# Order of states, inputs and lag copies in the state space group loop, and where its power vectors lie

## The chip, the cores and the metric

The kernel runs on one core of one Trainium2 chip. Five engines run programs of their own and meet only at semaphores: TensorE (PE, with its weight loads shown as PEld), VectorE (DVE), ScalarE (ACT), GpSimd (POOL) and SyncE (SP). The metric is the device time of one execution in microseconds. The kernel before took 3051.56 us, the median of three runs that lay between 3043.96 and 3056.59 us.

## The reference

Two networks follow each other on 256 tokens of width 1024. The first has two layers (an mLSTM or RG-LRU mixer with cross-attention, and a feed-forward block that gathers expert rows). The second has two layers of feed-forward, mixer, feed-forward. The change lies in the mixer of the second network's first layer, a diagonal complex state space model with 64 groups of 16 channels and 64 states. Cut to what matters:

```
u = (h @ w_in).reshape(bsz, seq, 64, 16)
abar = exp(dt * a)                                  # complex, one per state
bu   = einsum('blgh,gph->blgp', u, f * b)           # inputs
st   = scan(abar, bu)                               # states over the sequence
y    = Re(einsum('blgp,ghp->blgh', st, c)) + d_skip * u
z    = gelu(y) * sigmoid(gelu(y) @ w_glu + b_glu)
out  = z @ w_out
```

## The kernel before, in words

The sequence of 256 tokens is cut into 64 steps of 4 tokens. What passes inside a step of four goes through "lag" matrices, what passes from step to step goes through a scan of 64 columns. The 4096 states lie as 128 partitions x 32 columns, and the loop handles 4 of the 32 columns at a time: 8 groups, `for g in range(S5_G + 1)`, with the end of group g - 1 in round g. A complex state turns by an angle at each step. The kernel turns inputs back by the angle, scans with the real magnitude alone, and turns the result forward again.

Ahead of the loop stands a front part. `dve_s5_params` works out vectors of 128x32: f (V_FR, V_FI) and the powers 1 to 4 of abar (V_AR, V_AI), most of them in the SBUF buffer skT. `dve_times` multiplies the b tables by f and by three powers on DVE (four calls of four instructions), `c_power` the c tables by powers 1 and 2 on DVE and by 3 and 4 on POOL. ACT meanwhile copies the columns of u into place (`u4_rows`, L1484). It then waits for the b tables, builds the first matrices (`act_s5_bbz`, L1508) and copies the third part of u. PE's first round opens with 48 small matmuls that are there only to keep it active (6 in later rounds).

In round g each engine runs its program in the order in which it is written:
- PE: `drive(g)` (6 matmuls to keep active, then 16 that give the inputs s.v g), `rows_b(g+1)` (L1406), `lags(g)` (the tile s.k g; it needs the c matrices that POOL copied), `outputs(g-1)` (into acc; it needs state g-1 from POOL and the lag copies of g-1 from DVE).
- DVE: t1, t2 of group g (L1777, L1778, the inputs turned back), q1, q2 of group g-1 (L1784, L1785, the scan turned forward), four lag copies of group g (L1499), eight scans of group g (L1791).
- POOL: the inputs of group g (L1642, L1644), the states of group g-1 (L1649, L1650), the c matrices for group g+1 (`pool_s5_cp`, L1604, which waits until outputs(g-1) has read the buffer), the angle of group g+2 (L1611), and, after ACT has rounded it (L1521, L1523), the turn (L1616).
- ACT: the weights of drive(g+1) (L1515), matrices of group g+2 (L1508), rounding, and the sines of group g+2 (L1531 to L1537), which wait for q2 of group g.

PSUM has eight banks. `ps` has four, which all tiles take in turn, so each tile of a round waits until the tile four earlier has been read: s.k g+1 waits for the lag copies of group g. `acc` has the other four. In the front part nothing uses them; in the loop outputs(g) fills half of bank g // 2.

The buffers and constants that the change names: `area(...)` is a piece of the SBUF buffer arena, `s5v(k)` is vector k of the state vectors, S5_J is 32.

Of the kernel before, what the change touches and what calls it, by code (L numbers as in the profile page):

```python
# [14 lines left out]
ALU = mybir.AluOpType  # L15
# [141 lines left out]
def build(nc, A, out, known):  # L157
# [6 lines left out]
    with ctx:  # L164
# [1453 lines left out]
        def pool_s5():  # L1618

            pool.wait_ge(dve_steps, count_of("x mid01"))  # L1620
            pool_s5_loads()
            pool.wait_ge(dve_steps, count_of("angle4"))
            pool_s5_ang(0)
            pool_s5_turn(0)
            pool.wait_ge(act_steps, count_of("cpu 0"))
            pool.wait_ge(dve_steps, count_of("s5 powers"))
            c_power(pool, PO, 3, p_tmp1, p_tmp2)
            pool_s5_ang(1)
            pool_s5_turn(1)
            c_power(pool, PO, 4, p_tmp1, p_tmp2)  # L1630
            pool.memset(cp, 0.0).then_inc(pool_steps, PO.step())
            pool.wait_ge(pool_steps, PO.n)
            pool.wait_ge(dve_steps, count_of("c powers"))
            pool_s5_cp(0)
            pool_s5_cp(1)
            for g in range(S5_G + 1):
                b = g % 2
                if g < S5_G:
                    if g >= 2:
                        pool.wait_ge(dve_steps, count_of(f"scan {g - 2}"))  # L1640
                    pool.wait_ge(dve_steps, count_of(f"t1 {g}"))
                    pool.tensor_tensor(w_in[:, b, 0, :, :], w_t1[:, b, 0, :, :], w_t1[:, b, 1, :, :], ALU.add).then_inc(pool_steps, PO.step(f"in re {g}"))  # L1642
                    pool.wait_ge(dve_steps, count_of(f"read s.v{g}"))
                    pool.tensor_tensor(w_in[:, b, 1, :, :], w_t2[:, b, 1, :, :], w_t2[:, b, 0, :, :], ALU.subtract).then_inc(pool_steps, PO.step(f"in im {g}"))  # L1644
                if g:
                    if g >= 3:
                        pool.wait_ge(pe_steps, count_of(f"s.y {g - 3}"))
                    pool.wait_ge(dve_steps, count_of(f"s.q {g - 1}"))
                    pool.tensor_tensor(w_st[:, 1 - b, 0, :, :], w_q1[:, 1 - b, 0, :, :], w_q1[:, 1 - b, 1, :, :], ALU.subtract).then_inc(pool_steps, PO.step())  # L1649
                    pool.tensor_tensor(w_st[:, 1 - b, 1, :, :], w_q2[:, 1 - b, 0, :, :], w_q2[:, 1 - b, 1, :, :], ALU.add).then_inc(pool_steps, PO.step(f"state {g - 1}"))  # L1650
                if g and g + 1 < S5_G:
                    pool_s5_cp(g + 1)
                if g + 2 < S5_G:
                    pool_s5_ang(g + 2)
                    pool_s5_turn(g + 2)

        def of_states(k):

            return s5v(k).unsqueeze(1).unsqueeze(3).to_broadcast([P, 2, S5_J, 16])

        def c_power(eng, E, k, t1, t2):

            eng.tensor_tensor(t1, cpu[:, 0, :, :, :], of_states(V_AR[k]), ALU.mult).then_inc(sems[E.who], E.step())
            eng.tensor_tensor(t2, cpu[:, 0, :, :, :], of_states(V_AI[k]), ALU.mult).then_inc(sems[E.who], E.step())
            eng.wait_ge(sems[E.who], E.n)
            eng.tensor_tensor(cpu[:, k, 0, :, :], t1[:, 0, :, :], t2[:, 1, :, :], ALU.add).then_inc(sems[E.who], E.step())
            eng.tensor_tensor(cpu[:, k, 1, :, :], t1[:, 1, :, :], t2[:, 0, :, :], ALU.subtract).then_inc(sems[E.who], E.step())
            eng.wait_ge(sems[E.who], E.n)

        def dve_times(re_out, im_out, src, ar, ai):  # L1670

            dve.tensor_tensor(d_tmp1, src, of_states(ar), ALU.mult).then_inc(dve_steps, VE.step())
            dve.tensor_tensor(d_tmp2, src, of_states(ai), ALU.mult).then_inc(dve_steps, VE.step())
            dve.wait_ge(dve_steps, VE.n)
            dve.tensor_tensor(re_out, d_tmp1[:, 0, :, :], d_tmp2[:, 1, :, :], ALU.subtract).then_inc(dve_steps, VE.step())
            dve.tensor_tensor(im_out, d_tmp1[:, 1, :, :], d_tmp2[:, 0, :, :], ALU.add).then_inc(dve_steps, VE.step())
            dve.wait_ge(dve_steps, VE.n)

        def dve_s5_params():
# [64 lines left out]
            for k, (i, j) in ((2, (1, 1)), (3, (2, 1)), (4, (2, 2))):  # L1744
# [6 lines left out]
                two(V_AI[k], V(V_AI[k]), V(V_TMP2), ALU.add)  # L1751
                done()
            found["s5 powers"] = (VE.who, VE.n)

        def dve_s5():
            n = "mid01"
            dve_pre(n)
            dve_s5_params()
            dve.wait_ge(s5_b, count_of("s5 b loaded"))
            dve_times(bbk[:, 3, 0, :, :], bbk[:, 3, 1, :, :], b_raw, V_FR, V_FI)  # L1760
            for k in range(1, S5_L):
                dve_times(bbk[:, 3 - k, 0, :, :], bbk[:, 3 - k, 1, :, :], bbk[:, 3, :, :, :], V_AR[k], V_AI[k])
                found["b powers"] = (VE.who, VE.n)
            dve.wait_ge(act_steps, count_of("cpu 0"))
            for k in (1, 2):
                c_power(dve, VE, k, d_tmp1, d_tmp2)
            found["c powers"] = (VE.who, VE.n)
            u4_rows(VE, 3)
            for g in range(S5_G + 1):
                b = g % 2  # L1770
                if g < S5_G:
                    dve.wait_ge(act_steps, count_of(f"cs {g}"))
                    v = cs[:, b, :, :, :]
                    o = tile_of(VE, f"s.v{g}").rearrange("p (a q c) -> p a q c", a=2, q=4)
                    if g >= 2:
                        dve.wait_ge(pool_steps, count_of(f"in im {g - 2}"))
                    dve.tensor_tensor(w_t1[:, b, :, :, :], o, v, ALU.mult).then_inc(dve_steps, VE.step(f"t1 {g}"))  # L1777
                    dve.tensor_tensor(w_t2[:, b, :, :, :], o, swapped(v), ALU.mult).then_inc(dve_steps, VE.step(f"read s.v{g}"))  # L1778
                if g:
                    v = cs[:, 1 - b, :, :, :]  # L1780
                    dve.wait_ge(dve_steps, count_of(f"scan {g - 1}"))
                    if g >= 3:
                        dve.wait_ge(pool_steps, count_of(f"state {g - 3}"))
                    dve.tensor_tensor(w_q1[:, 1 - b, :, :, :], w_sc[:, 1 - b, :, :, :], v, ALU.mult).then_inc(dve_steps, VE.step())  # L1784
                    dve.tensor_tensor(w_q2[:, 1 - b, :, :, :], w_sc[:, 1 - b, :, :, :], swapped(v), ALU.mult).then_inc(dve_steps, VE.step(f"s.q {g - 1}"))  # L1785
                if g < S5_G:
                    dve_s5_lags(g)
                    for part in range(2):
                        dve.wait_ge(pool_steps, count_of(f"in {('re', 'im')[part]} {g}"))
                        for q in range(4):  # L1790
                            dve.tensor_tensor_scan(w_sc[:, b, part, q, :], s5v(V_MAG4)[:, 4 * g + q:4 * g + q + 1].to_broadcast([P, S5_C]),  # L1791
                                                   w_in[:, b, part, q, :], 0.0, ALU.mult, ALU.add).then_inc(dve_steps, VE.step(f"scan {g}"))
            dve.wait_ge(act_steps, count_of("y gelu 1"))
            for q in range(3):
                for l in range(S5_L):
                    dst, src = y_rows(l, q, 0)
                    dve.tensor_copy(dst, src).then_inc(dve_steps, VE.step("y dve 0"))
# [12 lines left out]
            dve_post(n, acc_rows, 1.0, tmp_s5, "ffn02")  # L1810
# [277 lines left out]
```

## Time and profile before

| | |
|---|---|
| median of 3 runs | 3051.56 us (3043.96 to 3056.59) |
| profiled execution, its own time | 3055.92 us |
| span of the profile | 3054.2 us |
| PE busy | 2530.4 us, 83% |
| DVE busy | 1679.8 us, 55% |
| POOL busy | 1062.8 us, 35% |
| ACT busy | 799.8 us, 26% |
| mean granted TensorE clock | 0.908 |

The profile is one execution. Busy time counts instructions of an engine; its idle time before an instruction is put down to what released it last. The granted clock is the share of TensorE's full 2.4 GHz: 1.00 in a stretch is 2.4 GHz, 0.50 is 1.2 GHz, and values between are stretches that hold some of both. The state space mixer takes the span from about 2034 to 2264 us: its front part up to 2095, the loop to 2203, then the gate and output products.

### The profile page before, as it was taken

The page shows a single profiled execution, that of the slowest core. Times are in us where ns is not written, and L with a number is a line of the kernel's source. Part 1 is how long each engine was busy: PE and PEld are TensorE (multiplying, and loading weights), DVE is VectorE, ACT ScalarE, POOL GpSimd, SP SyncE. Part 2 cuts the span into 40 slices and gives each one's busy share as a digit, 9 for nine tenths or more (in the row PEclk, how much of TensorE's full clock was granted, in tenths as well). Part 3 has the DMA queues.
Part 4 walks back from the last instruction along what each step waited for, and adds up shares of the span by engine and source line. Part 5 has one row for each costly group of instructions (what it writes and reads, how often), then busy time and mean ns, then how long its engine had stood idle before and what let it go on. Part 6 is the DMA issues. An engine that isn't in the chain of part 4 may idle for free.

```text
span 3054.2 us, 29765 instructions
## 1 busy us (share of the span) xinstructions
PE 2530.4 (83%) x10910; PEld 1737.0 (57%) x10910; DVE 1679.8 (55%) x3410; ACT 799.8 (26%) x1499; POOL 1062.8 (35%) x1155
## 2 busy tenths in 40 slices
PE   8978777778778986877777778988889989997898
PEld 7847322223324664332222338976759979875797
DVE  0135666676753337766667635647525545464454
ACT  1111221212211412222121124334324343324332
POOL 0002777777772016777777740015300000000000
PEclk9979888998899998888888988998799989998899
DMA  6415999999995349999999973551036545521353
GB/s 226 152 62 204 404 409 409 407 405 403 409 404 195 115 154 399 409 407 408 400 409 403 409 301 124 200 162 53 16 116 193 193 135 190 202 88 42 125 188 116
DMA packets 322209, 766.87 MB, mean 251 GB/s; under 512 B 22064, under 2 KB 172496, under 8 KB 322064
## 3 DMA queue, kind: packets, MB, share of 16 engines
q0 software_dynamic: 150208, 546.77, 45.5%
q1 hardware_dynamic: 170576, 217.69, 21.9%
q8 instruction: 88, 1.44, 0.2%
q10 hardware_dynamic: 1280, 0.50, 0.1%
q14 instruction: 57, 0.47, 0.0%
HBM read 763.83 MB, written 1.05 MB: 250 GB/s over the span
## 4 chain that ended last, share of the span: by engine, by line
PE 53%; DVE 15%; DMA 14%; POOL 10%; issue 6%; ACT 2%; ACTq 0%; DVEq 0%; POOLq 0%
PE ps L267 29%; PE acc L267 23%; DMA arena<-in_peer_u,arena 13%; POOL arena L1029 9%; DVE arena L994 2%; DMA arena<-in_peer_v,arena 1%; DVE arena L925 1%; DVE arena L931 1%; DVE arena L927 1%; DVE arena L929 1%; DVE arena L923 1%; PE ps L325 1%; DVE arena L957 1%; DVE arena L961 0%; DVE arena L963 0%
## 5 line engine op out<-in xcount | busy, mean ns | idle before, releaser
L267 PE MATMUL acc<-arena 128*128 128x512 f32 (+2 forms) x2362 | 1044.9, 598 | 331.6 <-ACT arena L918 278.9
L267 PEld LDWEIGHTS acc<-arena 128*128 128x128 f32 x2362 | 464.1, 206 | 908.4 <-issue 579.7
L1029 POOL DMA_INDIRECT arena<-in_peer_u,arena x512 | 487.2, 952 | 420.2 <-DVE arena L967 242.1
L1029 POOL DMA_INDIRECT arena<-in_peer_v,arena x512 | 482.0, 941 | 207.1 <-issue 126.6
L299 DVE TENSOR_TENSOR lo_ring<-ring,hi_ring 128x2048 fp32r<-128x2048 f32 x132 | 302.0, 2289 | 329.7 <-ACT hi_ring L291 329.4
L994 DVE CUSTOM_DVE_ANT_0 arena<-arena,ps 128x1024 f32<-128x1024 f32 x256 | 306.7, 1219 | 214.3 <-DMA arena<-in_peer_u,arena 213.7
L994 DVE CUSTOM_DVE_ANT_0 arena<-arena,acc 128x1024 f32<-128x1024 f32 x256 | 305.6, 1219 | 191.6 <-DMA arena<-in_peer_u,arena 190.7
L267 PE MATMUL ps<-x_hi,hi_ring 128*128 128x256 f32 x1408 | 401.5, 285 | 11.1 <-DVE x_lo L1210 11.1
L267 PE MATMUL ps<-x_hi,lo_ring 128*128 128x256 f32 x1408 | 400.2, 284 | 0.0
L267 PE MATMUL ps<-x_lo,hi_ring 128*128 128x256 f32 x1408 | 398.0, 283 | 0.0
L291 ACT CAST hi_ring<-ring 128x2048 fp32r<-128x2048 f32 x132 | 250.6, 1900 | 435.8 <-PE ps L267 333.7
L267 PE MATMUL ps<-x_fm,ring 128*128 128x256 f32 (+2 forms) x1568 | 350.3, 385 | 6.7 <-ACT acc L981 2.2
L267 PEld LDWEIGHTS ps<-x_fm,ring 128*128 128x128 f32 (+2 forms) x1568 | 291.4, 187 | 60.9 <-issue 3.7
L267 PEld LDWEIGHTS ps<-x_hi,hi_ring 128*128 128x128 f32 x1408 | 270.1, 192 | 12.6 <-DVE x_lo L1210 12.6
L267 PEld LDWEIGHTS ps<-x_lo,hi_ring 128*128 128x128 f32 x1408 | 269.5, 191 | 0.0
L267 PEld LDWEIGHTS ps<-x_hi,lo_ring 128*128 128x128 f32 x1408 | 268.9, 191 | 0.0
L918 ACT ACTIVATE arena<-ident,arena 128x128 f32<-128x128 f32 x512 | 153.0, 387 | 311.0 <-DVE arena L1006 311.0
L267 PE MATMUL acc<-hi_ring,a_hi 128*128 128x512 f32 x352 | 138.5, 393 | 0.0
L267 PE MATMUL acc<-hi_ring,a_lo 128*128 128x512 f32 x352 | 138.0, 392 | 0.0
L267 PE MATMUL acc<-lo_ring,a_hi 128*128 128x512 f32 x352 | 138.0, 392 | 0.0
L912 ACT ACTIVATE arena<-arena 128x16 f32<-128x16 f32 x32 | 6.9, 216 | 392.4 <-DVE arena L994 392.4
L1967 POOL DMA_DIRECT2D rowb<-in_norm_post x6 | 3.4, 565 | 289.9 <-DVE stat L1249 270.4
(341 smaller groups left out, 2249.1 us busy)
## 6 DMA issues: line engine op xcount, KB each, us to landing
ring<-in_ffn_w SPq DMA_DIRECT2D x132, 1024.0 KB, 5.4
ring<-in_peer_w_q SPq DMA_DIRECT2D x16, 1024.0 KB, 5.4
ring<-in_mlstm_w_in SPq DMA_DIRECT2D x12, 1024.0 KB, 5.2
arena<-in_peer_u,arena POOLq DMA_INDIRECT x512, 8.9
arena<-in_peer_v,arena POOLq DMA_INDIRECT x512, 8.6
ring<-in_cv_w_in SPq DMA_DIRECT2D x8, 1024.0 KB, 5.5
ring<-in_rglru_w_in SPq DMA_DIRECT2D x8, 768.0 KB, 4.8
ring<-in_w_out SPq DMA_DIRECT2D x5, 1024.0 KB, 4.9
```

The costliest lines, as they stand in the source:

```text
L267: return pe.matmul(o, l, r, start=first, stop=last)
L291: act.copy(parts(name)[0], flat(name, ring, i % RING)).then_inc(act_steps, AC.step("hi " + name))
L299: dve.tensor_tensor(lo, flat(name, ring, i % RING), hi.bitcast(F32), ALU.subtract).then_inc(dve_steps, VE.step("lo " + name))
L325: i = pe.transpose(o[:, 256 * k + 128 * t:256 * k + 128 * t + 128], src(t, 2 * c + k), ident[:, :])
L918: act.activation(diag[:, k, :], ident[:, :], ACT.Copy, scale=coef[b][:, k:k + 1]).then_inc(act_steps, AC.step(f"diag {i}.{j - 1}.{k}"))
L923: dve.max(out_v[:, a], s).then_inc(dve_steps, VE.step())
L925: dve.max_index(out_i[:, a], out_v[:, a], s).then_inc(dve_steps, VE.step())
L927: dve.match_replace(s, out_v[:, a], s, NEG).then_inc(dve_steps, VE.step())
L929: dve.max(out_v[:, b], s).then_inc(dve_steps, VE.step())
L931: dve.max_index(out_i[:, b], out_v[:, b], s).then_inc(dve_steps, VE.step())
L994: dve.tensor_tensor_reduce(r, r, x_row(t), 1.0, 0.0, ALU.mult, ALU.add, dots[b][:, k:k + 1]).then_inc(dve_steps, VE.step(f"u used {g}"))
L1029: pool.indirect_dma_start(ring_[:, g % slots, :], None, table, bass.IndirectOffsetOnAxis(ix[j % 4][:, k:k + 1].bitcast(U32), 0), element_o ...
```

## The change

Three things change, all in the state space mixer. In the diff the increments of the engines' own semaphores, which end most lines, are cut off.

1. In each round DVE does q1, q2 of group g-1 first, then t1, t2 of group g, then the scans of group g, and the lag copies of group g last. In each round POOL does the two state instructions of group g-1 ahead of the two input instructions of group g.
2. `dve_times`, and `c_power` where DVE runs it, read their coefficient vectors from acc bank 3 in PSUM (`near_states`). One new DVE copy of 128x288 brings the nine vectors there from skT. POOL still reads them in SBUF.
3. The first temporary of these DVE functions, d_tmp1, lies in acc banks 1 and 2, not in arena.

```
-        d_tmp1, d_tmp2 = area(0, 2, S5_J, 16), area(1024, 2, S5_J, 16)
+        d_tmp1 = acc[:, 1:3, :].rearrange("p a (j h) -> p a j h", h=16)
+        d_tmp2 = area(1024, 2, S5_J, 16)
...
             for g in range(S5_G + 1):
                 b = g % 2
+                if g:
+                    if g >= 3:
+                        pool.wait_ge(pe_steps, count_of(f"s.y {g - 3}"))
+                    pool.wait_ge(dve_steps, count_of(f"s.q {g - 1}"))
+                    pool.tensor_tensor(w_st[:, 1 - b, 0, :, :], w_q1[:, 1 - b, 0, :, :], w_q1[:, 1 - b, 1, :, :], ALU.subtract)
+                    pool.tensor_tensor(w_st[:, 1 - b, 1, :, :], w_q2[:, 1 - b, 0, :, :], w_q2[:, 1 - b, 1, :, :], ALU.add)
                 if g < S5_G:
...
-                if g:
-                    if g >= 3:
-                        pool.wait_ge(pe_steps, count_of(f"s.y {g - 3}"))
-                    pool.wait_ge(dve_steps, count_of(f"s.q {g - 1}"))
-                    pool.tensor_tensor(w_st[:, 1 - b, 0, :, :], w_q1[:, 1 - b, 0, :, :], w_q1[:, 1 - b, 1, :, :], ALU.subtract)
-                    pool.tensor_tensor(w_st[:, 1 - b, 1, :, :], w_q2[:, 1 - b, 0, :, :], w_q2[:, 1 - b, 1, :, :], ALU.add)
...
+        def near_states(k):
+
+            return acc[:, 3, S5_J * (k - 7):S5_J * (k - 7) + S5_J].unsqueeze(1).unsqueeze(3).to_broadcast([P, 2, S5_J, 16])
+
         def c_power(eng, E, k, t1, t2):
...
-            eng.tensor_tensor(t1, cpu[:, 0, :, :, :], of_states(V_AR[k]), ALU.mult)
-            eng.tensor_tensor(t2, cpu[:, 0, :, :, :], of_states(V_AI[k]), ALU.mult)
+            states = near_states if E is VE else of_states
+            eng.tensor_tensor(t1, cpu[:, 0, :, :, :], states(V_AR[k]), ALU.mult)
+            eng.tensor_tensor(t2, cpu[:, 0, :, :, :], states(V_AI[k]), ALU.mult)
...
-            dve.tensor_tensor(d_tmp1, src, of_states(ar), ALU.mult)
-            dve.tensor_tensor(d_tmp2, src, of_states(ai), ALU.mult)
+            dve.tensor_tensor(d_tmp1, src, near_states(ar), ALU.mult)
+            dve.tensor_tensor(d_tmp2, src, near_states(ai), ALU.mult)
...
             found["s5 powers"] = (VE.who, VE.n)
+            dve.wait_ge(dve_steps, count_of("acc ffn00 read"))
+            dve.tensor_copy(acc[:, 3, 0:288], skT[:, :, :].rearrange("p a b -> p (a b)")[:, 224:512])
+            dve.wait_ge(dve_steps, VE.n)
...
             for g in range(S5_G + 1):
                 b = g % 2
+                if g:
+                    v = cs[:, 1 - b, :, :, :]
+                    dve.wait_ge(dve_steps, count_of(f"scan {g - 1}"))
+                    if g >= 3:
+                        dve.wait_ge(pool_steps, count_of(f"state {g - 3}"))
+                    dve.tensor_tensor(w_q1[:, 1 - b, :, :, :], w_sc[:, 1 - b, :, :, :], v, ALU.mult)
+                    dve.tensor_tensor(w_q2[:, 1 - b, :, :, :], w_sc[:, 1 - b, :, :, :], swapped(v), ALU.mult)
                 if g < S5_G:
...
-                if g:
-                    v = cs[:, 1 - b, :, :, :]
-                    dve.wait_ge(dve_steps, count_of(f"scan {g - 1}"))
-                    if g >= 3:
-                        dve.wait_ge(pool_steps, count_of(f"state {g - 3}"))
-                    dve.tensor_tensor(w_q1[:, 1 - b, :, :, :], w_sc[:, 1 - b, :, :, :], v, ALU.mult)
-                    dve.tensor_tensor(w_q2[:, 1 - b, :, :, :], w_sc[:, 1 - b, :, :, :], swapped(v), ALU.mult)
-                if g < S5_G:
-                    dve_s5_lags(g)
                     for part in range(2):
                         dve.wait_ge(pool_steps, count_of(f"in {('re', 'im')[part]} {g}"))
                         for q in range(4):
                             dve.tensor_tensor_scan(w_sc[:, b, part, q, :], s5v(V_MAG4)[:, 4 * g + q:4 * g + q + 1].to_broadcast([P, S5_C]),
                                                    w_in[:, b, part, q, :], 0.0, ALU.mult, ALU.add)
+                    dve_s5_lags(g)
```

A round of the loop on DVE, in the kernel before (ps is the tile read, arena the SBUF buffer; L1777 and L1778 are t1 and t2, L1784 and L1785 q1 and q2, L1499 the lag copies, L1791 the scans):

```order
L1777 TENSOR_TENSOR arena<-ps,arena 128x512 [waits pool_steps,pe_steps,act_steps]
L1778 TENSOR_TENSOR arena<-ps,arena 128x512
L1784 TENSOR_TENSOR arena<-arena 128x512 [waits pool_steps,dve_steps]
L1785 TENSOR_TENSOR arena<-arena 128x512
L1499 COPY arena<-ps 32x512 [waits pe_steps]
L1499 COPY arena<-ps 32x4x96
L1791 SCALAR_TENSOR_TENSOR arena<-mix_fm,arena 128x64 [waits pool_steps]
L1791 SCALAR_TENSOR_TENSOR arena<-mix_fm,arena 128x64 x3
```

The same round on DVE in the changed kernel (q1 and q2 are L1785 and L1786, t1 and t2 L1793 and L1794, the scans L1798, the lag copies L1500):

```order
L1785 TENSOR_TENSOR arena<-arena 128x512 [waits pool_steps,dve_steps]
L1786 TENSOR_TENSOR arena<-arena 128x512
L1793 TENSOR_TENSOR arena<-ps,arena 128x512 [waits pool_steps,pe_steps,act_steps]
L1794 TENSOR_TENSOR arena<-ps,arena 128x512
L1798 SCALAR_TENSOR_TENSOR arena<-mix_fm,arena 128x64 [waits pool_steps]
L1798 SCALAR_TENSOR_TENSOR arena<-mix_fm,arena 128x64 x3
L1500 COPY arena<-ps 32x512 [waits pe_steps]
L1500 COPY arena<-ps 32x4x96
```

The forward turn of the last group no longer stands behind the wait for PE's tile s.v g, and the lag copies no longer stand ahead of the scans.

On POOL, from the c matrices of one round to those of the next, before (L1604 the c matrices, L1611 the angle, L1616 the turn, L1642 and L1644 the inputs, L1649 and L1650 the states):

```order
L1604 COPY arena<-arena 64x20x16
L1611 TENSOR_TENSOR arena<-mix_fm,t_row 128x256 [waits act_steps,pool_steps]
L1616 TENSOR_TENSOR arena<-arena 128x256 [waits act_steps]
L1642 TENSOR_TENSOR arena<-arena 128x256 [waits dve_steps]
L1644 TENSOR_TENSOR arena<-arena 128x256 [waits dve_steps]
L1649 TENSOR_TENSOR arena<-arena 128x256 [waits dve_steps,pe_steps]
L1650 TENSOR_TENSOR arena<-arena 128x256
L1604 COPY arena<-arena 64x20x16 [waits pool_steps,pe_steps]
```

And in the changed kernel (L1605 the c matrices, L1612 the angle, L1617 the turn, L1643 and L1644 the states, L1649 and L1651 the inputs):

```order
L1605 COPY arena<-arena 64x20x16
L1612 TENSOR_TENSOR arena<-mix_fm,t_row 128x256 [waits act_steps,pool_steps]
L1617 TENSOR_TENSOR arena<-arena 128x256 [waits act_steps]
L1643 TENSOR_TENSOR arena<-arena 128x256 [waits dve_steps,pe_steps]
L1644 TENSOR_TENSOR arena<-arena 128x256
L1649 TENSOR_TENSOR arena<-arena 128x256 [waits dve_steps]
L1651 TENSOR_TENSOR arena<-arena 128x256 [waits dve_steps]
L1605 COPY arena<-arena 64x20x16 [waits pool_steps,pe_steps]
```

The states, for which PE waits, now come two instructions earlier on POOL, and the inputs two later. PE's and ACT's programs keep their order.

On DVE in the front part, the first call of dve_times in the changed kernel, behind the last vectors:

```order
L1690 TENSOR_TENSOR mix_fm<-mix_fm,skT 128x32
L1761 COPY acc<-skT 128x288 [waits dve_steps]
L1678 TENSOR_TENSOR acc<-arena,acc 128x1024 [waits s5_b,dve_steps]
L1679 TENSOR_TENSOR arena<-arena,acc 128x1024
L1681 TENSOR_TENSOR arena<-acc,arena 128x512 [waits dve_steps]
L1682 TENSOR_TENSOR arena<-acc,arena 128x512
```

Before, L1672 and L1673 stood for the two products and L1675 and L1676 for the sum and difference, with arena and skT in the place of each acc, and without the copy.

## Rows read from the trace of the kernel before

**Rows 1.** Windows: busy us of each engine (x), granted clock, DMA share, GB/s.
```profile
2034.00:2095.00 61.00, 38.97 (x178) 33.66 (x178) 54.43 (x95) 33.74 (x98) 33.24 (x22) 0.79 0.40 112
2095.00:2203.00 108.00, 99.00 (x655) 85.97 (x654) 65.03 (x157) 38.75 (x88) 49.03 (x78) 0.77 0.03 11
```

**Rows 2.** The same view, three shorter stretches of the loop.
```profile
2102.00:2112.20 10.20, 10.20 (x88) 7.83 (x86) 7.40 (x18) 3.52 (x8) 4.22 (x6) 1.00 0.00 0
...
2114.80:2127.50 12.70, 12.70 (x60) 11.59 (x60) 4.18 (x13) 3.48 (x9) 4.55 (x8) 0.50 0.01 2
2127.50:2139.10 11.60, 11.32 (x98) 9.28 (x96) 8.09 (x18) 5.10 (x13) 6.78 (x11) 1.00 0.01 1
```

**Rows 3.** Timeline of PE: start, us, line, names, xcount, idle before and releaser.
```profile
2114.76 0.66 PE L267 MATMUL acc<-mix_fm,arena 128*128 128x64 f32 x2 [2.55 <-DVE arena L1499]
...
2119.91 1.49 PE L267 MATMUL ps<-ident 128*128 128x256 bf16 x6
...
2130.02 0.41 PE L267 MATMUL acc<-mix_fm,arena 128*128 128x64 f32 x2 [0.24 <-POOL arena L1650]
...
2132.72 0.82 PE L267 MATMUL ps<-ident 128*128 128x256 bf16 x6
...
2136.08 0.62 PE L267 MATMUL ps<-arena 128*32 128x128 f32 x4
...
2140.97 0.58 PE L267 MATMUL acc<-mix_fm,arena 128*128 128x64 f32 x2 [1.91 <-POOL arena L1650]
...
2183.96 0.82 PE L267 MATMUL ps<-ident 128*128 128x256 bf16 x6
...
2201.63 3.73 PE L267 MATMUL ps<-x_fm,ring 128*128 128x256 f32 x8
```

**Rows 4.** Timeline of POOL in the round that ends with the 1.91 us wait.
```profile
2132.95 1.85 POOL L1604 COPY arena<-arena 64x320 f32<-64x320 f32 x4 [3.08 <-PE acc L267]
2134.88 0.61 POOL L1611 TENSOR_TENSOR arena<-mix_fm,t_row 128x256 f32<-128x256 f32 x1
2136.47 0.72 POOL L1616 TENSOR_TENSOR arena<-arena 128x256 f32<-128x256 f32 x1 [0.98 <-ACT arena L1523]
2137.16 1.17 POOL L1642 TENSOR_TENSOR arena<-arena 128x256 f32<-128x256 f32 x1
...
2139.42 0.72 POOL L1649 TENSOR_TENSOR arena<-arena 128x256 f32<-128x256 f32 x1
```

**Rows 5.** Timeline of DVE in the same round.
```profile
2135.36 0.69 DVE L1777 TENSOR_TENSOR arena<-ps,arena 128x512 f32<-128x512 f32 x1 [1.73 <-issue]
...
2137.67 1.21 DVE L1785 TENSOR_TENSOR arena<-arena 128x512 f32<-128x512 f32 x1
2139.10 2.02 DVE L1499 COPY arena<-ps 32x512 f32<-32x512 f32 x4 [0.22 <-PE ps L267]
2141.15 1.56 DVE L1791 TENSOR_TENSOR_SCAN arena<-mix_fm,arena 128x64 f32<-128x64 f32 x8
```

**Rows 6.** Groups by line, DVE, 2060 to 2095: busy us, mean ns, idle before.
```profile
L1673 DVE TENSOR_TENSOR arena<-arena,skT 128x1024 f32<-128x1024 f32 x4 | 8.1, 2020 | 0.0
...
L1663 DVE TENSOR_TENSOR arena<-arena,skT 128x1024 f32<-128x1024 f32 x2 | 2.4, 1224 | 0.1
...
L1666 DVE TENSOR_TENSOR arena<-arena 128x512 f32<-128x512 f32 x2 | 1.4, 692 | 0.1
```

**Rows 7.** Timelines of DVE, ACT and PE in the front part.
```profile
2034.55 2.36 DVE L1245 TENSOR_TENSOR arena<-acc,rowb 128x1024 f32<-128x1024 f32 x2 [17.96 <-PE acc L267]
...
2060.61 1.22 DVE L1672 TENSOR_TENSOR arena<-arena,skT 128x1024 f32<-128x1024 f32 x1
...
2074.92 8.97 ACT L1484 COPY mix_fm<-ps 32x128 f32<-32x128 f32 x32
2087.09 1.68 ACT L1508 COPY arena<-arena 64x256 f32<-64x256 f32 x4 [3.20 <-DVE arena L1676]
...
2093.41 6.98 PE L267 MATMUL ps<-ident 128*128 128x256 bf16 x48 [2.62 <-ACT mix_fm L1484]
```

More of the change, by code:

```diff
@@ L1637, in pool_s5 @@
                 b = g % 2
+                if g:
+                    if g >= 3:
+                        pool.wait_ge(pe_steps, count_of(f"s.y {g - 3}"))
+                    pool.wait_ge(dve_steps, count_of(f"s.q {g - 1}"))
+                    pool.tensor_tensor(w_st[:, 1 - b, 0, :, :], w_q1[:, 1 - b, 0, :, :], w_q1[:, 1 - b, 1, :, :], ALU.subtract).then_inc(pool_steps, PO.step())
+                    pool.tensor_tensor(w_st[:, 1 - b, 1, :, :], w_q2[:, 1 - b, 0, :, :], w_q2[:, 1 - b, 1, :, :], ALU.add).then_inc(pool_steps, PO.step(f"state {g - 1}"))
                 if g < S5_G:
@@ L1644, in pool_s5 @@
                     pool.tensor_tensor(w_in[:, b, 1, :, :], w_t2[:, b, 1, :, :], w_t2[:, b, 0, :, :], ALU.subtract).then_inc(pool_steps, PO.step(f"in im {g}"))
-                if g:
-                    if g >= 3:
-                        pool.wait_ge(pe_steps, count_of(f"s.y {g - 3}"))
-                    pool.wait_ge(dve_steps, count_of(f"s.q {g - 1}"))
-                    pool.tensor_tensor(w_st[:, 1 - b, 0, :, :], w_q1[:, 1 - b, 0, :, :], w_q1[:, 1 - b, 1, :, :], ALU.subtract).then_inc(pool_steps, PO.step())
-                    pool.tensor_tensor(w_st[:, 1 - b, 1, :, :], w_q2[:, 1 - b, 0, :, :], w_q2[:, 1 - b, 1, :, :], ALU.add).then_inc(pool_steps, PO.step(f"state {g - 1}"))
                 if g and g + 1 < S5_G:
@@ L1659, in of_states @@
             return s5v(k).unsqueeze(1).unsqueeze(3).to_broadcast([P, 2, S5_J, 16])
+        def near_states(k):
+            return acc[:, 3, S5_J * (k - 7):S5_J * (k - 7) + S5_J].unsqueeze(1).unsqueeze(3).to_broadcast([P, 2, S5_J, 16])
         def c_power(eng, E, k, t1, t2):
-            eng.tensor_tensor(t1, cpu[:, 0, :, :, :], of_states(V_AR[k]), ALU.mult).then_inc(sems[E.who], E.step())
-            eng.tensor_tensor(t2, cpu[:, 0, :, :, :], of_states(V_AI[k]), ALU.mult).then_inc(sems[E.who], E.step())
+            states = near_states if E is VE else of_states
+            eng.tensor_tensor(t1, cpu[:, 0, :, :, :], states(V_AR[k]), ALU.mult).then_inc(sems[E.who], E.step())
+            eng.tensor_tensor(t2, cpu[:, 0, :, :, :], states(V_AI[k]), ALU.mult).then_inc(sems[E.who], E.step())
             eng.wait_ge(sems[E.who], E.n)
@@ L1670, in dve_times @@
         def dve_times(re_out, im_out, src, ar, ai):
-            dve.tensor_tensor(d_tmp1, src, of_states(ar), ALU.mult).then_inc(dve_steps, VE.step())
-            dve.tensor_tensor(d_tmp2, src, of_states(ai), ALU.mult).then_inc(dve_steps, VE.step())
+            dve.tensor_tensor(d_tmp1, src, near_states(ar), ALU.mult).then_inc(dve_steps, VE.step())
+            dve.tensor_tensor(d_tmp2, src, near_states(ai), ALU.mult).then_inc(dve_steps, VE.step())
             dve.wait_ge(dve_steps, VE.n)
@@ L1753, in dve_s5_params @@
             found["s5 powers"] = (VE.who, VE.n)
+            dve.wait_ge(dve_steps, count_of("acc ffn00 read"))
+            dve.tensor_copy(acc[:, 3, 0:288], skT[:, :, :].rearrange("p a b -> p (a b)")[:, 224:512]).then_inc(dve_steps, VE.step())
+            dve.wait_ge(dve_steps, VE.n)
         def dve_s5():
@@ L1770, in dve_s5 @@
                 b = g % 2
+                if g:
[3 more added lines that the diff above has]
+                        dve.wait_ge(pool_steps, count_of(f"state {g - 3}"))
+                    dve.tensor_tensor(w_q1[:, 1 - b, :, :, :], w_sc[:, 1 - b, :, :, :], v, ALU.mult).then_inc(dve_steps, VE.step())
+                    dve.tensor_tensor(w_q2[:, 1 - b, :, :, :], w_sc[:, 1 - b, :, :, :], swapped(v), ALU.mult).then_inc(dve_steps, VE.step(f"s.q {g - 1}"))
                 if g < S5_G:
@@ L1778, in dve_s5 @@
                     dve.tensor_tensor(w_t2[:, b, :, :, :], o, swapped(v), ALU.mult).then_inc(dve_steps, VE.step(f"read s.v{g}"))
-                if g:
-                    v = cs[:, 1 - b, :, :, :]
-                    dve.wait_ge(dve_steps, count_of(f"scan {g - 1}"))
-                    if g >= 3:
-                        dve.wait_ge(pool_steps, count_of(f"state {g - 3}"))
-                    dve.tensor_tensor(w_q1[:, 1 - b, :, :, :], w_sc[:, 1 - b, :, :, :], v, ALU.mult).then_inc(dve_steps, VE.step())
-                    dve.tensor_tensor(w_q2[:, 1 - b, :, :, :], w_sc[:, 1 - b, :, :, :], swapped(v), ALU.mult).then_inc(dve_steps, VE.step(f"s.q {g - 1}"))
-                if g < S5_G:
-                    dve_s5_lags(g)
                     for part in range(2):
```

## The prediction

> **What bounds the kernel now.** I read the windows of the mixer first, to see what its stages are worth, then the timelines of PE, POOL and DVE side by side over two rounds, then the front part. The mixer's front part takes 61 us and its loop 108 of the span's 3054.2, and in neither is DMA a limit: its share in the loop is 0.03 [rows 1]. What stands behind the loop follows PE's own end of it, so a microsecond saved here should reach the end.
>
> In the loop PE looks nearly always busy (99.0 of 108 us), but the granted clock is 0.77 [rows 1]. The shorter windows show why: 10.2 us without a gap at clock 1.00, then a gap of 2.55 us, then 12.7 us at 0.50 (1.2 GHz), then 11.6 at 1.00 again [rows 2, 3]. Another gap, of 1.91 us, ends that fast stretch [rows 3], and the pattern stands three times more, with gaps of about 2 us. No stretch at the full clock in the loop ended without one; the first lasted about 15 us from its rise at 2097. So a gap costs twice: itself, and the slow stretch behind it.
>
> A round at the full clock needs from PE 3.36 us up to the lags (2132.72 to 2136.08), 2.98 us for them (to 2139.06: the next start less its wait of 1.91) and 2.70 us for the outputs (2130.02 to 2132.72): 9.04 us. Five rounds took 2183.96 - 2119.91 = 64.05 us, 12.81 each [rows 3].
>
> What makes the gap is POOL. It starts the c matrices 0.23 us into the round and ends them at 2.1; then come the angle, ACT's rounding and the turn, until 4.44; then the two inputs, 2.26 us (1.17 for what takes 0.72 alone), and the two states, after which PE goes on at 8.25 (2140.97), 1.91 late [rows 4, 3]. Beside the inputs DVE runs q1 and q2 at about 1.2 us each, where t1, of their size, takes 0.69 [rows 5].
>
> **The loop, part by part.** No instruction is added in a round and PE's and ACT's order stays. I count from the start of a round at the full clock.
>
> POOL's states move ahead of the inputs: 4.44 + 1.55 (2139.42 to 2140.97, states and PE's reaction) = 5.99, and PE wants them at 6.34. The gap goes, with 0.35 us to spare, if q2 is done by 4.44. The inputs, now behind, run from about 5.9 to 7.8 (1.9 us, between 1.44 and 2.26); of the eight scans (1.56 us) half are left then, until 8.6; the lag copies, 2.02 us, have their tile since 6.34 and end at 10.6; q1 and q2, 1.3 to 2.4 us, at 11.9 to 13.0, that is 2.9 to 4.0 in the next round [rows 3 to 5]. That is 0.4 to 1.5 before 4.44. What is queued behind q1 and q2 on DVE are t1, t2, and for them wait POOL's inputs: they end at 5.4 at the latest, and POOL is free at 5.9. PE's lags of the next group need the bank that the lag copies free at 10.6 - 9.04 = 1.6 and the c matrices at 2.1, both ahead of 3.36. ACT's sines wait for q2 and the turn; the turn is last, as before.
>
> So a round becomes 9.04 us by this; I take 9.3, because 0.35 us are eaten by one collision of POOL with DVE. First outputs: the lags of group 1 end at 2112.20, now the outputs follow at once and take 2.70 instead of the slow 5.15, so that the round ends at 2114.9, not 2119.91: 5.0 us. Five rounds: 5 x (12.81 - 9.3) = 17.5 us. The tail, from 2183.96 to 2201.63, is 17.67 us now [rows 3]. In the new order PE is done with outputs 6 after 2.4 + 2.98 + 2.7 = 8.1, but the last state comes after q2 of group 6 (3.5), two states (4.9), inputs (6.7), scans (7.6), copies (9.6), q1 and q2 (10.9), states: 12.4. The gap is over 4 us and the last outputs run slowly, 5.15: 17.5. The tail gives nothing. That gap's slow stretch may reach 2 us into the gate product, which now begins sooner behind it: minus 1 us. Loop: 5.0 + 17.5 - 1 = 21.5 us.
>
> **The front part.** The 24 DVE instructions of the power tables run from 2060.61 [rows 7]. The first ones collide with POOL's c powers: a 128x1024 product takes 2.02 us in the mean, and 1.22 where POOL does nothing, a 128x512 one 0.69 [rows 6]. The Trainium skill, page "SBUF — State Buffer", section "Who interferes with whom", has DVE's second SBUF input go through a read port that GpSimd shares, by an exclusive lock, and an instruction with one SBUF input contend with nobody; L1777, with one input in PSUM, keeps 0.69. In the new form each of the 24 has one SBUF input. A call of dve_times should take 2 x 1.22 + 2 x 0.69 = 3.8 us; four calls, 15.3, from 2061.1 to 2076.4, where before ACT got them at 2087.09.
>
> What is late next is ACT. Its columns of u run from 2074.92 to 2083.89, and start after POOL's turn of group 1. POOL loses its collisions too (an angle takes 0.61 alone [rows 4]); I estimate 2.1 us from that. ACT then ends at 2081.8, builds its matrices at once instead of waiting 3.20 us, and PE's 48 small matmuls start 5.3 us earlier than 2093.41 [rows 7]. DVE's c powers end at 2084 and its 16 copies of u near 2089, before the 2095 at which PE asks for them.
>
> No row shows DVE writing PSUM, nor reading it with one word repeated. The nearest row is L1245, 128x1024 from acc, two in 2.36 us [rows 7], so I take 1.22. The other end is the 2.02 of the collided form, for which a call takes 5.4 us and DVE's copies end near 2099: PE gets its inputs 4 us later than planned, and the front gives 1 us. Nothing bounds it below the uncollided form, since that is one pass over the same elements. The new copy of 128x288 lies between 0.4 and 0.7 us by the 0.69 of a 128x512 one; it is hidden, as DVE has 5 us to spare ahead of ACT.
>
> Sum: 21.5 + 5.3 = 26.8, say 27 us. The profiled execution took 3055.92 us, so it would take 3028.9. It lies 4.4 above the median of the runs; against 3051.56 this gives 3024.8, and I say 3025.
>
> **Rivals.** *The clock falls without a gap.* The Trainium skill, page "TensorE: Matmul & The Clock Gate", section "A second HAM failure mode: psum-queue depth-cycling", tells of a kernel whose clock went up and down because PE idled briefly between groups while it cycled through PSUM banks, as this loop does with its four. In this trace the window 2102 to 2112.2 speaks against it (the same small matmuls, clock 1.00, no gap), and that the outputs were not among them speaks for it. Then only the gaps go: 2.55 and four of about 1.7, 9 us, and with the front's 5.3 the time is 3051.6 - 14 = 3037.
>
> *The wait only moves.* POOL's and DVE's instructions with two SBUF inputs are 1.3 (q) + 1.6 (scans) + 1.85 + 0.61 + 0.72 + 1.45 + 1.44 = 9.0 us of a 9.04 us round. If each collides, the states come 0.7 to 1 us late each round and the clock keeps falling. By the lock that the skill's SBUF page describes this is what would happen if all of them took it; rows 4 and 5 show it for q against inputs, while POOL's copies took 1.85 us beside scans. Then the loop gives about 6 us, the front 5: 3041.
>
> *The front gives nothing*, PSUM forms being slow: 21.5 alone, 3030.
>
> *Slower.* The lag copies now stand behind the scans, which stand behind POOL's inputs, and PE's next lags need their bank. If the copies end more than 1.8 us later than I reckon, a gap opens ahead of the lags in every round. With a gap in each there is no fast stretch; a round at 1.2 GHz takes 1.85 x 9.04 = 16.7 us, against 12.81, and six rounds add 23 us, less 5 from the front: 3070. Against it speak the 1.8 us, and that a slow PE makes room for DVE.
>
> **Chances.** The forecast 0.60 (3020 to 3031), clock falls without a gap 0.17, the wait moves 0.08, no gain in front 0.10, slower 0.05. About 0.5%, 15 us, is what a measurement of this kernel can tell from no change. The forecast and the front's rival are faster than 3036.3, as is a third of the first rival: 0.76. The rest of the first two is within 0.5%: 0.19. Slower 0.05. The range that leaves out 2 in 10 reaches from 3016, where all of 32 us comes and the run is a quick one, to 3041.
>
> **What would show it.** In the changed profile PE's waits for POOL's states should be under 0.3 us in rounds 1 to 5 and the granted clock of the loop's first 70 us 1.00; a new gap of 4 us before the last outputs; L1678 and L1679 near 1.22 us, L1681 and L1682 near 0.69; ACT without a wait for the b tables. I am wrong if the clock falls in the middle of the loop behind no gap, if PE waits for the lag copies, or if L1678 takes 2 us.

## The result, and the profile after

The changed kernel took 3020.72 us, the median of four runs (3016.55 to 3022.94), against 3053.37 for four runs of the kernel before: ratio 0.9894, 95% interval 0.9879 to 0.9909, 32.6 us less. The forecast was 3025, 27 us less. Its profiled execution took 3019.64 us with a span of 3017.9, 36.3 less than before.

Where these 36.3 us went can be read from four marks in both timelines: the mixer's start (the first product of the post-norm ahead of it, L1245), PE's 48 small matmuls, the gate product, and the next L1245.

| us | before | after | less by | forecast |
|---|---|---|---|---|
| ahead of the mixer | 2034.55 | 2031.66 | 2.9 | 0 |
| front part, to the 48 matmuls | 58.86 | 52.15 | 6.7 | 5.3 |
| loop, to the gate product | 108.22 | 84.45 | 23.8 | 22.5 |
| gate and output products | 61.71 | 61.73 | 0.0 | -1 |
| behind the mixer | | | 2.9 | 0 |

The mixer gives 30.5 us of the 36.3. The stages around it hold the same instructions, and differ by 2.9 us on either side. No run ties these 5.8 us to the change, and the prediction did not count them.

PE's timeline after answers to [rows 3] (start, us, names, xcount, idle before and releaser):

```profile
2083.81 7.01 PE L267 MATMUL ps<-ident 128*128 128x256 bf16 x48 [3.50 <-ACT mix_fm L1485]
...
2096.27 0.83 PE L267 MATMUL ps<-ident 128*128 128x256 bf16 x6
...
2105.28 0.82 PE L267 MATMUL ps<-ident 128*128 128x256 bf16 x6
...
2111.94 0.41 PE L267 MATMUL acc<-mix_fm,arena 128*128 128x64 f32 x2 [0.32 <-POOL arena L1644]
...
2114.64 0.82 PE L267 MATMUL ps<-ident 128*128 128x256 bf16 x6
...
2150.64 0.82 PE L267 MATMUL ps<-ident 128*128 128x256 bf16 x6
...
2163.12 0.66 PE L267 MATMUL acc<-mix_fm,arena 128*128 128x64 f32 x2 [4.20 <-POOL arena L1644]
...
2168.26 3.73 PE L267 MATMUL ps<-x_fm,ring 128*128 128x256 f32 x8
```

One wait of 0.32 us is left in the middle; the five rounds from 2105.28 take 45.36 us, 9.07 each, where they took 64.05. The tail from 2150.64 takes 17.62 us, as before (17.67), with the forecast gap ahead of the last outputs. PE's gaps in the loop add up to 8.9 us before and to 4.5 after, so only 4.4 of the 23.8 us are idle time that went; the other 19.4 came from the clock. The windows view (busy us of PE, PEld, DVE, ACT, POOL, then granted clock, DMA share, GB/s) shows the clock:

```profile
2090.66:2153.00 62.34, 62.02 (x540) 53.73 (x538) 46.92 (x111) 34.77 (x81) 38.36 (x62) 1.00 0.01 1
...
2163.10:2174.00 10.90, 8.88 (x32) 7.63 (x32) 8.34 (x22) 4.45 (x6) 0.97 (x2) 0.57 0.26 98
2174.15:2200.40 26.25, 26.17 (x120) 22.72 (x120) 2.08 (x3) 2.56 (x7) 0.00 (x0) 1.00 0.36 120
```

The full clock, 2.4 GHz, now lasts 62 us in one piece, where [rows 2] had it change every 10 to 15 us. In the loop it falls only at the 4.20 us of the tail, and is back when the gate product goes on.

In the front part the groups by line on DVE (busy us, mean ns, idle before) answer to [rows 6]:

```profile
L1678 DVE TENSOR_TENSOR acc<-arena,acc 128x1024 f32<-128x1024 f32 x4 | 4.9, 1229 | 0.1
L1679 DVE TENSOR_TENSOR arena<-arena,acc 128x1024 f32<-128x1024 f32 x4 | 4.9, 1213 | 0.0
...
L1681 DVE TENSOR_TENSOR arena<-acc,arena 128x512 f32<-128x512 f32 x4 | 2.8, 692 | 0.1
...
L1761 DVE COPY acc<-skT 128x288 f32<-128x288 f32 x1 | 0.5, 461 | 0.0
```

POOL's timeline there; the same two instructions took 2.90 and 1.59 us before, beside DVE's instructions with two SBUF inputs:

```profile
2057.84 1.93 POOL L1669 TENSOR_TENSOR arena<-arena,skT 128x1024 f32<-128x1024 f32 x1 [4.69 <-DVE mix_fm L1690]
...
2061.74 1.27 POOL L1672 TENSOR_TENSOR arena<-arena 128x512 f32<-128x512 f32 x1
```

And ACT's, which answers to [rows 7]:

```profile
2068.46 8.99 ACT L1485 COPY mix_fm<-ps 32x128 f32<-32x128 f32 x32
2077.48 1.69 ACT L1509 COPY arena<-arena 64x256 f32<-64x256 f32 x4
```

ACT builds its matrices without a wait (3.20 us before), and its columns of u start 36.80 us after the mixer's start, where they started at 40.37.

### The profile page after: what moved, and what is told of

The parts are those of the page before. It is cut to its first block, busy times and chain, and to the rows that moved or that the text cites. A ratio compares the mean times of both kernels' runs of the same rounds, so it can differ in the third digit from the quotient of the medians.

```text
span 3017.9 us, 29767 instructions
## 1 busy us (share of the span) xinstructions
PE 2506.1 (83%) x10910; PEld 1716.1 (57%) x10910; DVE 1668.3 (55%) x3411; ACT 799.7 (26%) x1499; POOL 1050.5 (35%) x1155
## 4 chain that ended last, share of the span: by engine, by line
PE 54%; DVE 14%; DMA 13%; POOL 11%; issue 6%; ACT 2%; ACTq 0%; DVEq 0%; POOLq 0%
PE ps L267 30%; PE acc L267 24%; DMA arena<-in_peer_u,arena 12%; POOL arena L1029 10%; DVE arena L994 3%; DVE arena L925 1%; DVE arena L931 1%; DVE arena L927 1%; DMA arena<-in_peer_v,arena 1%; DVE arena L929 1%; PE ps L325 1%; DVE arena L923 1%; DVE arena L957 1%; DVE arena L1245 0%; ACT mix_fm L1485 0%
## 5 line engine op out<-in xcount | busy, mean ns | idle before, releaser
L267 PEld LDWEIGHTS acc<-arena 128*128 128x128 f32 x2362 | 457.1, 202 | 907.2 <-issue 579.3
```

What stands on the lines that cost most here:

```text
L267: return pe.matmul(o, l, r, start=first, stop=last)
```

## The experiments

The theory: PE's gap was POOL's, POOL's delay came from its order and from collisions with DVE, and the slow clock behind each gap cost more than the gap. The rivals: the clock falls for another reason; one of the two orders would have done; the front part's gain hangs on something else than the second SBUF input. The runs were made on several chips, and on two of them the kernel before took 3194 and 3207 us. So the experiments are compared by the mixer's stages between the four marks, where the same instructions take the same time on each (the 120 matmuls of the gate product at the full clock: 26.17 us on each). Where no ratio is given, the numbers are those of a single execution.

**Front part alone.** The loops of `pool_s5` and `dve_s5` are those of before, all else is the changed kernel.

> Only the front part is changed (vectors and first temporary in PSUM), the loop keeps the old order. Theory (DVE and POOL wait for each other at the SBUF port, ACT was held by the b tables): the front part, from the post-norm's first product to PE's 48 small matmuls, falls from 58.9 us to about 52.2, the loop stays at 108 +- 2 with its four gaps and slow stretches; total 6 to 7 us less than before, ratio 0.998. Rival (the front gain would have been eaten by PE's clock or a later wait, and the loop alone made the difference): front near 58, total unchanged.

Measured: ratio 0.9978 (0.9962 to 0.9994), front part 52.07 us, loop 108.04. The four gaps of the kernel before are all there (2.55, 1.88, 1.89 and 2.14 us; 2.55, 1.91, 1.89 and 2.14 before), and one of 0.88 us behind them, where 0.19 stood. The theory holds. In the profiled execution the gate part took 64.8 us instead of 61.7: the clock came back only within the gate product, whose 120 matmuls took 29.1 us instead of 26.2.

**Loop alone.** The other half: power tables in SBUF as before, the new orders.

> Only the loop's orders on DVE and POOL are changed, the power tables stay in SBUF. Theory: front 58.9 us as before, loop from 108.2 to about 84.5 us with rounds of 9.0 to 9.4 us at clock 1.00; total 23 to 24 us less than before, ratio 0.992. Rival (the two parts need each other, since an earlier DVE gives the loop its lead): the loop stays above 90 us.

Measured: ratio 0.9907 (0.9886 to 0.9928), front 58.89, loop 84.72, gate part 61.73. The two parts need nothing of each other: 58.86 - 52.07 = 6.8 and 108.22 - 84.72 = 23.5 us add to 30.3, and the changed kernel has 30.5.

**One engine's order alone.** First `pool_s5` as changed with `dve_s5` as before, then the other way round; the power tables as before in both.

> Only POOL's order in the loop is changed (states ahead of inputs), DVE's is old. Theory: q1, q2 come after t1, t2 and end near 5.0 to 5.3 us into a fast round, so the states end near 6.7 and PE waits 0.3 to 0.6 us a round instead of 1.9 in every second; if a gap so small leaves the clock alone the loop takes about 88 us. Rival (both orders are needed to close the gap): gaps of 1 us and more remain, the clock keeps falling, loop 100 us or more.

> Only DVE's order in the loop is changed (q1, q2 first, lag copies last), POOL's is old. Theory: the inputs no longer collide with q1, q2 and take 1.45 instead of 2.26 us, so the states end near 7.4 us into a fast round and PE waits about 1.0 us; loop between 92 and 105 us, with slow stretches if 1 us is enough to bring the clock down. Rival (DVE's order is what counts): gap gone, loop near 85 us.

Measured: with POOL's order alone the loop took 104.9 us, with DVE's alone 103.8. The second lies in the range of its theory, the first does not. PE's timeline with POOL's order alone:

```profile
2273.24 0.82 PE L267 MATMUL ps<-ident 128*128 128x256 bf16 x6
...
2280.53 0.41 PE L267 MATMUL acc<-mix_fm,arena 128*128 128x64 f32 x2 [0.95 <-POOL arena L1643]
...
2283.23 0.82 PE L267 MATMUL ps<-ident 128*128 128x256 bf16 x6
...
2290.45 0.41 PE L267 MATMUL acc<-mix_fm,arena 128*128 128x64 f32 x2 [0.88 <-POOL arena L1643]
...
2294.38 1.49 PE L267 MATMUL ps<-ident 128*128 128x256 bf16 x6
```

I had expected 0.3 to 0.6 us there and a clock that holds. The gap was 0.95 us, since q1 stands behind t1 and t2 and met POOL's turn (DVE's L1784 took 1.15 us), and the clock fell behind the second gap: the small matmuls at 2294.38 take 1.49 us instead of 0.82. So the rival was right here (it had asked for 1 us and more): both orders are needed. With DVE's order alone the inputs shrink from 1.17 to 0.73 us, as the theory says, and PE still waits 1.28 us in the middle (L1650, the states, end at 2281.48 and PE goes on at 2281.63), which brings the clock down in every second round. A gap of 0.9 to 1.3 us in place of 1.9 gave 3.3 and 4.5 us of 23.5.

**The gap filled.** The kernel before, its order untouched:

```
                 if g:
+                    if g < S5_G:
+                        keep_active(acc[:, 3, 256:512], 16)
                     outputs(g - 1)
```

> The kernel before, with 16 more of the small bf16 matmuls between a round's lags and its outputs, in rounds 1 to 7; no order is changed and no wait is removed. Theory (the slow clock is caused by the gaps and is two thirds of the loop's loss): at the full clock the 16 take 1.75 us of a gap of 1.9 that is there anyway, the clock stays at 1.00 in the middle of the loop, rounds take about 11 us and the loop 95 to 98 us instead of 108, though PE does more work. Rival (what was lost is PE's waiting itself, or the small matmuls bring the clock down anyway): the clock still falls and the loop takes 108 us or more.

Measured: loop 102.17 us, between the two. The windows say why:

```profile
2264.00:2279.00 15.00, 14.96 (x82) 12.06 (x83) 5.78 (x15) 6.84 (x17) 6.30 (x10) 0.59 0.00 1
2283.50:2327.00 43.50, 43.50 (x379) 37.27 (x378) 27.63 (x64) 20.29 (x48) 26.68 (x40) 1.00 0.01 1
```

In the first round 16 matmuls were too few, a gap of 0.70 us stayed and a slow stretch followed. From then on no gap was left and the clock stayed at 1.00 for all of the middle. Four rounds there took 10.87 us each, though PE did 1.8 us more work in each than in a kernel whose rounds took 12.81. This shows the price most clearly: no engine's work for the states was touched, the gaps were only filled, and the 1.9 us a round come from the clock alone.

**One gap put in.** The changed kernel, round 4 of POOL alone:

```
                     pool.wait_ge(dve_steps, count_of(f"s.q {g - 1}"))
+                    if g == 4:
+                        for _ in range(3):
+                            pool.tensor_tensor(w_st[:, 1 - b, 0, :, :], w_q1[:, 1 - b, 0, :, :], w_q1[:, 1 - b, 1, :, :], ALU.subtract)
+                            pool.wait_ge(pool_steps, PO.n)
```

> The changed kernel, with POOL's first state instruction done three times over ahead of itself in round 4 alone, 0.7 us each. Theory: one gap of about 2.1 us ahead of outputs 3, a slow stretch of 10 to 14 us behind it, and a loop of 84.5 + 2.1 + 5 to 6.5 = 91.5 to 93 us. Rival (the clock falls for another reason): only the 2.1 us, 86.6.

```profile
2255.00:2290.00 35.00, 34.67 (x300) 29.46 (x300) 27.57 (x64) 18.05 (x44) 21.78 (x36) 1.00 0.00 1
...
2293.10:2305.00 11.90, 11.86 (x56) 11.22 (x57) 6.47 (x16) 3.11 (x9) 6.58 (x11) 0.50 0.01 1
2306.00:2325.00 19.00, 19.00 (x164) 16.11 (x164) 12.08 (x31) 10.76 (x21) 9.68 (x17) 1.00 0.00 1
```

Measured: a gap of 2.30 us, 12 us at 1.2 GHz behind it, loop 92.96 us. That is 8.5 us more than the changed kernel for 2.3 us of idle time: the gap makes the clock fall, and the slow stretch costs about 6 us (0.3 of the rest is a longer gap in the tail, 4.53 us).

**Lag copies ahead of the scans again**, q1 and q2 still first (`dve_s5_lags(g)` moved back above the scans).

> The changed kernel with one part of the order undone: DVE's lag copies again ahead of the scans. Theory (PE waits for POOL's chain of c matrices, angle, turn and states, and DVE has over 1 us to spare): the loop stays within 1.5 us of 84.5. Rival (the copies have to be last, since the scans would then end too late for q1, q2 and the states): PE waits 0.5 us or more in each round and the loop takes 90 us or more.

Measured: loop 87.25 us, outside both numbers. PE waits 0.34 us in each round and the rounds are 9.38 us. POOL's and DVE's timelines of one of these rounds:

```profile
2280.92 2.56 POOL L1605 COPY arena<-arena 64x320 f32<-64x320 f32 x4 [1.71 <-PE acc L267]
2283.55 0.61 POOL L1612 TENSOR_TENSOR arena<-mix_fm,t_row 128x256 f32<-128x256 f32 x1
```

```profile
2281.54 0.76 DVE L1785 TENSOR_TENSOR arena<-arena 128x512 f32<-128x512 f32 x1
2282.22 0.93 DVE L1786 TENSOR_TENSOR arena<-arena 128x512 f32<-128x512 f32 x1
```

The end of the scans, q1 and q2 now run beside POOL's c matrices, which take 2.56 us instead of 1.75. The angle takes 0.61 us instead of 0.93 to 1.00, and in sum the states come about 0.4 us later. DVE had not run out of time: q2 ends 2.5 us into this round, before the 3.6 of the changed kernel. So the copies' place is worth 2.8 us because it decides which of POOL's instructions q1 and q2 meet. It is no condition for the full clock, which even held behind a first gap of 0.82 us.

**Vectors in PSUM, first temporary in SBUF.**

```
-        d_tmp1 = acc[:, 1:3, :].rearrange("p a (j h) -> p a j h", h=16)
-        d_tmp2 = area(1024, 2, S5_J, 16)
+        d_tmp1, d_tmp2 = area(0, 2, S5_J, 16), area(1024, 2, S5_J, 16)
```

> The changed kernel with the coefficient vectors in PSUM but the first temporary back in SBUF. Theory (it is the second SBUF input that makes DVE and POOL wait for each other): the products keep 1.22 us, the sums and differences, now with two SBUF inputs, take 0.9 to 1.6 us instead of 0.69 while POOL works, and the front part takes 52.5 to 54.5 us. Rival (PSUM for the vectors is all that matters): front 52.1 and all four at their times of the changed kernel.

```profile
L1681 DVE TENSOR_TENSOR arena<-arena 128x512 f32<-128x512 f32 x4 | 5.4, 1351 | 0.0
L1677 DVE TENSOR_TENSOR arena<-arena,acc 128x1024 f32<-128x1024 f32 x4 | 4.9, 1220 | 0.1
...
L1680 DVE TENSOR_TENSOR arena<-arena 128x512 f32<-128x512 f32 x4 | 4.8, 1200 | 0.1
```

Measured: front part 53.03 us, inside the range. The two products, one input in PSUM, keep 1.22 us beside POOL's work; the sum and difference, both inputs in SBUF again, take 1.20 and 1.35 us in the mean, where they take 0.69 and 0.68 with one in PSUM. The theory holds, and the rule of the Trainium skill's page "SBUF — State Buffer" ("Who interferes with whom"), that two SBUF inputs on DVE contend with GpSimd and one does not, agrees with this trace; the temporary's place is worth 0.9 us of the 6.7.

**A better version.** Two places stood out: PE spends 7 us on the 48 matmuls after it has been idle, since their bank comes free late, and the tail's 4.20 us gap.

```
-                keep_active(o, 48 if g == 0 else 6)
+                keep_active(o, 6)
...
-            rows_b(0)
             pe.wait_ge(dve_steps, count_of("acc ffn00 read"))
+            keep_active(acc[:, 0, :], 18)
+            rows_b(0)
+            keep_active(acc[:, 0, :], 46)
...
+                    if g == S5_G:
+                        keep_active(acc[:, 3, 256:512], 22)
                     outputs(g - 1)
```

In the tail version DVE also does, in round 7 alone, q1 and q2 of group 7 ahead of its lag copies.

> The changed kernel as it is, on the same chip as the next three, to compare with them: front 52.1 us, loop 84.5, mixer 198.3; ratio to before 0.989 to 0.991.

> The changed kernel, with the small bf16 matmuls moved: instead of 48 ahead of the first inputs (7 us, which only the bank of s.v 0 allowed to begin late) there are 18 ahead of the first b tiles and 46 behind them, into acc bank 0, which is free then. Theory: the first inputs wait for the last copies of u, not for the 48 matmuls, and come 4 to 5 us earlier than the 59.0 us after the mixer's start that they take in the changed kernel, at clock 1.00; mixer 193.5 to 194.5 us. Rival (the clock falls while PE waits for the copies, and the first rounds run slowly): mixer 197 or more.

> The changed kernel, with q1, q2 of the last group ahead of its lag copies, and 22 small matmuls ahead of the last outputs. Theory: the gap before the last outputs shrinks from 4.2 to about 0.3 us of idle, they start 1.3 to 1.6 us earlier and take 2.7 instead of 5.15 us; from the start of round 7 to the gate product 17.6 falls to 13.5 to 14 us; mixer 194 to 195. Rival (the tail waits for ACT and DVE copies of y, and the gate product begins as late as before): mixer 197 or more.

> Both of the two before together. Theory: they lie one behind the other and add, 8 to 9.5 us below the changed kernel, mixer 189 to 190.5 us, ratio to before 0.986 to 0.988. Rival (one of them takes the other's lead): 4 to 5 us only.

| us | changed again | warm front | tail | both |
|---|---|---|---|---|
| mixer's start to the gate product | 136.72 | 131.74 | 135.19 | 130.24 |
| gate and output products | 61.71 | 64.61 | 62.84 | 60.65 |
| mixer | 198.43 | 196.35 | 198.03 | 190.89 |

The forecasts for the mixer were 193.5 to 194.5 us for the warm front, 194 to 195 for the tail and 189 to 190.5 for both: all three fell short. The warm front brought the first inputs to 54.1 us after the mixer's start instead of 59.0, as forecast, and that holds up to the gate product. But in its profile 2.9 us were lost in the gate product. The tail's last outputs ran at the full clock, but the gate product then waited 2.41 us for DVE's copies of y, which now end later than PE, and the clock fell there instead. The gate product began 1.5 us earlier, but the mixer's 198.03 us are what the rival gave (197 or more). With both, measured: 3013.33 us, ratio to before 0.9875 (0.9858 to 0.9891), the changed kernel beside it 3024.11, 0.9898 (0.9882 to 0.9915). It beats the kernel before clearly. Against the changed kernel the intervals of the two ratios overlap; the medians lie 10.8 us apart, and the mixer is 7.5 us shorter in the profile. PE's timeline of the last rounds with both:

```profile
2153.07 2.56 PE L267 MATMUL acc<-ident 128*128 128x256 bf16 x22
2155.76 0.44 PE L267 MATMUL acc<-mix_fm,arena 128*128 128x64 f32 x2
...
2161.06 3.37 PE L267 MATMUL ps<-x_fm,ring 128*128 128x256 f32 x8 [2.41 <-DVE x_fm L1815]
2165.87 26.17 PE L267 MATMUL ps<-x_fm,ring 128*128 128x256 f32 x120 [1.44 <-DVE x_fm L1820]
```

And the windows of the gate product, with the warm front alone and with both:

```profile
2167.70:2196.80 29.10, 29.05 (x120) 24.82 (x120) 2.08 (x3) 2.53 (x7) 0.00 (x0) 0.90 0.33 109
```

```profile
2165.80:2192.00 26.20, 26.13 (x120) 22.77 (x120) 2.09 (x4) 2.52 (x6) 0.00 (x0) 1.00 0.36 121
```

The same 120 matmuls differ by 2.9 us by whether the clock comes back before them or among them.

## Why the prediction was right, point by point

- **The bound.** PE's gaps and the slow clock behind them. Filling the gaps and putting one in showed it from both sides, so the clock's part is shown, not only argued. The prediction counts one gap too many: there are four of about 1.9 us or more (2.55, 1.91, 1.89, 2.14) and two of about 0.2. Their sum, 9 us, is right.
- **States ahead of the inputs on POOL.** Forecast: the gap goes, 0.35 us to spare, a round of 9.3 us. Measured 9.0 in most rounds and 9.36 in one, 5 x (12.81 - 9.07) = 18.7 us instead of 17.5. The collision came in every round, but ate only the 0.35 us to spare, as the timeline of POOL shows (c matrices and angle, in the round with the wait and in the next):

```profile
2105.51 2.21 POOL L1605 COPY arena<-arena 64x320 f32<-64x320 f32 x4 [2.17 <-PE acc L267]
2107.80 0.93 POOL L1612 TENSOR_TENSOR arena<-mix_fm,t_row 128x256 f32<-128x256 f32 x1
...
2114.87 1.75 POOL L1605 COPY arena<-arena 64x320 f32<-64x320 f32 x4 [1.71 <-PE acc L267]
2116.70 1.00 POOL L1612 TENSOR_TENSOR arena<-mix_fm,t_row 128x256 f32<-128x256 f32 x1
```

  The angle takes 0.93 to 1.00 us beside q2, where it took 0.61; only in the first of these rounds did q1 and q2 meet the c matrices too. So the 0.3 us a round that I added on top were needed once, not five times. That q2 ends ahead of the turn was the condition, and the run with POOL's order alone shows what is lost without it.
- **First outputs and tail.** 5.0 us forecast, 14.05 - 9.01 = 5.04 measured; the tail nothing, 0.05 measured, with its gap at 4.20 us. The 1 us for a slow gate product did not come in this profile. In eight of the twelve experiments 1.4 to 2.9 us of it did, so that this term came out at nothing is partly luck.
- **Front part.** Both PSUM directions on DVE cost what the SBUF form costs alone, 1.23 and 1.21 us, so the lower end of the range was right. The term that was mis-sized is POOL's share: I took 2.1 us, and showed only the angle's 0.61 us for it. POOL's four instructions of the c powers took 2.90, 2.91, 1.59 and 1.71 us before and 1.93, 1.93, 1.27 and 1.28 after, 2.7 less, and the angle behind them 0.61 instead of 1.47. That is the 3.6 us by which ACT starts earlier. With the 3.2 us of ACT's wait this is the 6.7.
- **Rivals.** In the loop the clock does not fall without a gap: 62 us at 1.00 with the outputs in it, while all four banks are cycled. What the Trainium skill tells of another kernel ("TensorE: Matmul & The Clock Gate", "A second HAM failure mode: psum-queue depth-cycling"), a clock that goes up and down while PE cycles through PSUM banks with short idle times, did not happen in this one. PE never waited for the lag copies, which was the slower case. The wait did not move either. DVE and POOL do collide, but in the changed kernel within the time to spare. The lag copies in their old place come nearest to this rival, with 0.34 us a round, and the clock held.
- **The signs.** PE's waits were to be under 0.3 us: one was 0.32. The clock was to be 1.00 from the loop's start: its first 3.3 us, among the 48 small matmuls, still ran at 1.2 GHz. The others came as said.

All in all 30.5 us in the mixer against 26.8 forecast. The 32.6 of the medians hold about 2 us more, from outside the mixer, which no run ties to the change.

## What to carry to other kernels

Look at what the granted clock does behind a short wait of PE before you price the wait: here 2.3 us of idle time cost 8.5. Each of the two reorderings alone brought less than a fifth of what both brought, so changes that do little alone can be worth trying together. And where DVE and GpSimd work side by side, an operand moved from SBUF to idle PSUM can free both engines: here DVE's products went from 2.02 us in the mean to 1.22, and GpSimd's from 2.90 to 1.93.

## What the runs showed of the hardware

- In this loop short gaps already bring the clock down, but not each time: behind 0.70 and 0.88 us it fell, behind 0.96 us twice, behind 0.82 and the first 0.95 us it did not, and behind 0.32 to 0.35 us, thirteen times in these runs, never.
- The length of a gap alone does not decide it. Ahead of the output product PE waited 1.85 to 1.95 us in each of the fourteen kernels, behind a gate product without a gap, and the clock never fell. In the changed kernel (PE's timeline, then the windows view):

```profile
2202.18 27.70 PE L267 MATMUL acc<-ring,arena 128*128 128x512 f32 x64 [1.86 <-DVE arena L1815]
```

```profile
2200.40:2229.90 29.50, 27.70 (x64) 12.08 (x64) 5.28 (x3) 5.97 (x6) 0.00 (x0) 1.00 0.45 142
```

  A gap of 1.36 us at 548.5 us in the kernel before, among matmuls of 512 columns, left the clock at 1.00 as well. What sets these places apart from the loop was not tested.
- DVE writes 128x1024 fp32 to PSUM in 1.23 us and reads a vector there with each word repeated 16 times at the same rate, as from SBUF alone.
- A 128x1024 tensor_tensor on GpSimd takes 1.93 us beside DVE's instructions with one SBUF input, and 2.38 to 2.91 beside those with two.
